# Hybrid encoder step on eight cores: weight conversion spread over two groups, casts on two more engines, eight PSUM banks for gate and up

## Time and profile before

| | |
|---|---|
| times of 3 runs | 7601.93, 8012.99 and 8454.6 us, median 8012.99 |
| profiled execution | 7586.13 us, span of its slowest core 7585.1 us |
| spans of the 8 cores | 7554.7 to 7585.1 us, granted clock 0.958 to 0.965 |
| first group (31.4 to 1022.7 us) | 991.3 us |
| fifth group, the same block number without conversion | 767.4 us |
| second group (1022.7 to 1821.9 us) | 799.2 us |
| last group, the sample tokens (from 6749 us) | 836.1 us |

### The profile page before, as it was taken

The page is one execution under the profiler, slowest core; times in us unless marked ns, Lnnn a source line. Parts: engine busy times, 40 slices in busy tenths (PEclk is TensorE's granted clock), DMA queues, the critical chain, the costliest instruction groups (busy, mean ns, idle before and its releaser), DMA issues.

```text
span 7585.1 us, 114887 instructions; the slowest of 8 cores (7554.7 to 7585.1 us)
## 1 busy us (share of the span) xinstructions
PE 6630.0 (87%) x39776; PEld 3525.2 (46%) x39776; DVE 2912.0 (38%) x5057; ACT 2651.3 (35%) x4204; POOL 1403.3 (19%) x1750
## 2 busy tenths in 40 slices
PE   5777788989899998989898989899999989896777
PEld 2333334454444445454444454544444454555666
DVE  4545534343333343333434343433343433433332
ACT  1412315151524335261414152524333351614343
POOL 1112111202111121212121212121121212122121
PEclk9899999999999999999999999999999999998888
DMA  8699762424233342424242424243343424256666
GB/s 264 216 310 306 224 206 85 146 86 157 97 121 122 115 154 69 147 73 160 97 146 98 158 89 142 95 148 116 109 134 103 148 70 149 77 181 213 208 222 200
DMA packets 452258, 1130.56 MB, mean 149 GB/s; under 512 B 38384, under 2 KB 166128, under 8 KB 451696
## 3 DMA queue, kind: packets, MB, share of 16 engines
q1 hardware_dynamic: 433568, 1059.23, 43.5%
q0 software_dynamic: 18128, 63.97, 2.2%
HBM read 973.12 MB, written 149.95 MB: 148 GB/s over the span
## 4 chain that ended last, share of the span: by engine, by line
PE 61%; DVE 11%; ACT 10%; issue 7%; DMA 5%; POOL 4%; SPq 2%; DVEq 0%; ACTq 0%; POOLq 0%
PE psb L542 14%; PE psb L522 12%; PE psb L518 11%; PE psb L756 5%; POOL tC L533 4%; PE psb L889 3%; PE psb L986 3%; PE psb L1007 3%; DVE tA L528 2%; PE psb L696 2%; ACT tA L531 2%; ACT eT L1065 2%; SPq L270 1%; PE psb L1166 1%; ACT tq L759 1%
## 5 line engine op out<-in xcount | busy, mean ns | idle before, releaser
L533 POOL TENSOR_TENSOR tC<-tA,rstdT 128x512 f32<-128x512 f32 (+1 forms) x792 | 954.4, 1205 | 4198.5 <-ACT tA L531 4081.0
L522 PE MATMUL psb<-hT,wring 128*128 128x512 bf16 (+1 forms) x6336 | 1430.9, 369 | 132.3 <-DVE BIG L536 126.6
L518 PE MATMUL psb<-hT,wring 128*128 128x512 bf16 (+1 forms) x6336 | 1434.5, 369 | 87.2 <-DVE tA L528 78.6
L542 PE MATMUL psb<-BIG,wring 128*128 128x512 bf16 (+1 forms) x6336 | 1322.5, 370 | 43.8 <-DVE wring L412 38.6
L531 ACT ACTIVATE tA<-tA 128x512 f32<-128x512 f32 (+1 forms) x792 | 479.8, 606 | 2218.3 <-DVE tA L528 2217.9
L536 DVE TENSOR_TENSOR BIG<-psb,tC 128x512 bf16<-128x512 f32 (+1 forms) x792 | 524.2, 662 | 1757.8 <-POOL tC L533 1757.8
L522 PEld LDWEIGHTS psb<-hT,wring 128*128 128x128 bf16 x6336 | 588.1, 98 | 895.0 <-issue 355.3
L518 PEld LDWEIGHTS psb<-hT,wring 128*128 128x128 bf16 x6336 | 618.9, 98 | 785.6 <-issue 133.4
L542 PEld LDWEIGHTS psb<-BIG,wring 128*128 128x128 bf16 x6336 | 621.1, 98 | 735.4 <-issue 76.9
L528 DVE TENSOR_TENSOR tA<-psb,rstdT 128x512 f32<-128x512 f32 (+1 forms) x792 | 515.7, 651 | 164.7 <-ACT rstdT L485 164.6
L994 ACT ACTIVATE eT<-psb 128x1024 bf16<-128x1024 f32 (+2 forms) x640 | 532.7, 892 | 106.4 <-PE psb L986 57.5
(11 more groups left out here) (179 smaller groups left out, 6233.0 us busy)
## 6 DMA issues: line engine op xcount, KB each, us to landing
wring<-wsc SPq DMA_DIRECT2D x1280, 512.0 KB, 3.9
wsc<-wring SPq DMA_DIRECT2D x160, 512.0 KB, 9.4
vb<-w_gate SPq DMA_DIRECT2D x66, 512.0 KB, 9.7
vb<-w_up SPq DMA_DIRECT2D x66, 512.0 KB, 10.7
vb<-w_down SPq DMA_DIRECT2D x66, 512.0 KB, 12.3
vb<-cbk SPq DMA_DIRECT2D x64, 512.0 KB, 5.1
vb<-cbv SPq DMA_DIRECT2D x64, 512.0 KB, 4.5
vb<-w_in SPq DMA_DIRECT2D x36, 512.0 KB, 11.6
```

The source lines that it names most:

```text
L518: P.add("pe", lambda kc=kc, bg=bg, wg=wg, fl=fl: nc.tensor.matmul(psb[bg][:, 0:T], wg[:, kc, fl * 128:(fl + 1) * 128], hT[:, kc, 0:T], sta ...
L522: P.add("pe", lambda kc=kc, bu=bu, wu=wu, fl=fl: nc.tensor.matmul(psb[bu][:, 0:T], wu[:, kc, fl * 128:(fl + 1) * 128], hT[:, kc, 0:T], sta ...
L533: P.add("pool", lambda ts=ts: nc.gpsimd.tensor_tensor(out=tC[ts][:, 0:T], in0=tA[ts][:, 0:T], in1=rstdT[:, 0:T], op=ALU.mult), [("t", ts, ...
L542: P.add("pe", lambda: nc.tensor.matmul(psb[ab][:, 0:T], wd[:, fl, dcl * 128:(dcl + 1) * 128], aT[:, fc, 0:T], start=(fc == 0), stop=(fc == ...
```

## The change

- Conversion goes over two groups. In the first group every tile is still loaded as float32 and cast, but only the `in` and `out` tiles and those with an even index (`written_first`, 104 of 168) are written to `wsc`. The second group fetches those 104 from `wsc`, and loads, casts and writes the other 64 (56 full and 8 half-sized) itself.
- The fetches of the second group are issued 2 tiles ahead in `first_pass`. From the third group on, nothing of this changes.
- The staging area grows: 12 halves in the first group (parts of `kbT` too, in two pieces of 512 columns), 8 in the second.
- Of the two halves of a tile, VectorE casts the first. The second is cast by ScalarE, for `in` and `out` tiles by GpSimd.
- Gate and up use all eight banks: chunk `fc` has the pair `2 * (fc % 4)`.
- `o_transpose` of group B is put off by 4 tiles for `i = 0` and 6 otherwise (before: 2, 4, 6 and 6 for the four block numbers), in bank 4 for `i` 0 and 1. The last head's is after unit 5 of group A (before: 3), in bank 7. In group A it stands ahead of the normalization of the fourth unit, not behind it.

```diff
@@ staging and the two groups
+    late = [k_ for k_ in parts if k_[0] == "k" or (k_[0] == "v" and k_[2] > 0)]
+    early = late + [k_ for k_ in parts if k_ not in late]
...
+    def written_first(tid):
+        (l, name, idx) = cat_list[tid][0]
+        return name in ("in", "out") or idx % 2 == 0
+
+    def converts(n):
+        return n < NW or (n < NCONV and not written_first(n % NW))
+
+    def writes_back(n):
+        return written_first(n % NW) if n < NW else converts(n)
...
     def first_cast(n):
...
+                if hf == 0:
+                    P.add("dve", lambda: nc.vector.tensor_copy(out=dst, in_=buf), tk, [("w", s)])
+                elif name in ("in", "out"):
+                    P.add("pool", lambda: nc.gpsimd.tensor_copy(out=dst, in_=buf), tk, [("w", s)])
+                else:
+                    P.add("act", lambda: nc.scalar.copy(out=dst, in_=buf), tk, [("w", s)])
...
+    def cast_to(m):
+        while fp["cast"] < min(m, NCONV):
+            if converts(fp["cast"]):
+                first_cast(fp["cast"])
+            fp["cast"] += 1
+
     def first_pass(n):
-        while fp["load"] < min(n + LOOK + 3, NFIRST):
-            while fp["cast"] <= min(fp["load"] - 4, n + LOOK):
-                first_cast(fp["cast"])
-                fp["cast"] += 1
-            first_load(fp["load"])
+        while fp["load"] < min(n + LOOK + 3, NCONV):
+            cast_to(min(fp["load"] - 3, n + LOOK + 1))
+            if converts(fp["load"]):
+                first_load(fp["load"])
             fp["load"] += 1
...
+        cast_to(n + LOOK + 1)
+        while fp["back"] < min(n + LOOK, NCONV):
+            if writes_back(fp["back"]):
+                first_back(fp["back"])
             fp["back"] += 1
+        while fp["fetch"] < min(n + LOOK + 1, NCONV):
+            if not converts(fp["fetch"]):
+                fetch(fp["fetch"])
+            fp["fetch"] += 1
@@ def ffn
-                bg, bu = rot(), rot()
+                bg = 2 * (fc % 4)
+                bu = bg + 1
@@ def attn_prompt
-        def o_transpose(half, hh):
-            bt = 6
+        def o_transpose(half, hh, bt):
...
-                    deferred.append([idx + min(nk // 2, 6), o_transpose, (1, h)])
+                    lag = 4 if i == 0 else 6
+                    deferred.append([idx + lag, o_transpose, (1, h, 6 if lag <= nk // 2 else 4)])
...
+            if u == 3 and hp > 0:
+                o_transpose(0, hp - 1, 6)
             if u % 2 == 1:
...
-            if u == 3 and hp > 0:
-                o_transpose(0, hp - 1)
...
-            if idx == 4:
-                flush(10 ** 9)
-        o_transpose(0, 3)
+            if idx == 6:
+                for d_ in deferred:
+                    d_[1](1, 3, 7)
+                deferred.clear()
+        o_transpose(0, 3, 6)
```

More of the change, by code:

```diff
@@ L367, in build @@
     cat_list = list(cat.items())
-    NFIRST = len(cat_list)
+    NW = len(cat_list)
+    NCONV = 2 * NW
     LOOK = 2
-    stage = []
+    parts = {}
     for l_ in range(2):
         for k_ in range(3):
[L373 to L379, removed]
-    fp_halves = {}
+            parts[("v", l_, k_)] = (
+                [vbt[l_][:, 4 + 4 * k_:8 + 4 * k_].rearrange("p a h b -> p (a h b)")[:, 0:2048].bitcast(F32)],
+                [("vb", l_, 4 + 4 * k_ + q) for q in range(4)])
+        parts[("a", l_)] = ([vat[l_][:, 4:8].rearrange("p a h b -> p (a h b)")[:, 0:2048].bitcast(F32)],
+                            [("va", l_, 4 + q) for q in range(4)])
+        for p_ in range(2):
+            parts[("k", l_, p_)] = ([kbT[l_][:, 2 * p_ + a_, 1024:2048].bitcast(F32) for a_ in range(2)],
+                                    [("kbx", l_, p_)])
+    late = [k_ for k_ in parts if k_[0] == "k" or (k_[0] == "v" and k_[2] > 0)]
+    early = late + [k_ for k_ in parts if k_ not in late]
+    fp = {"load": 0, "cast": 0, "back": 0, "fetch": 0, 0: 0, 1: 0}
+    fp_halves = {}
+    def written_first(tid):
[5 more added lines that the diff above has]
+        return written_first(n % NW) if n < NW else converts(n)
     def tile_nel(n):
-        (l, name, idx), tid = cat_list[n]
+        (l, name, idx), tid = cat_list[n % NW]
         if name[0] == "d":
@@ L440, in wload @@
         wcount[0] += 1
-        s = n % NSLOT
-        if n < NFIRST:
-            if cat_list[n][1] != tid:
-                raise ValueError("weight order")
+        if cat_list[n % NW][1] != tid:
+            raise ValueError("weight order")
+        if n < NCONV:
             first_pass(n)
-            return s
-        while fp["back"] < NFIRST:
-            first_back(fp["back"])
-            fp["back"] += 1
-        dma("sp", wring[:, s, 0:nel], wsc[tid][:, 0:nel], [("ws", tid)], [("w", s)], ("w", s))
-        return s
+        else:
+            fetch(n)
+        return n % NSLOT
     nstate = {"bank": None, "pend": []}
@@ L737, in qk_job @@
             FT = ("t", ts, "B")
+            xtok = []
             if kind == "ka":
```

58 lines of the change are left out of this document (34 added, 24 removed).

## The result

The changed kernel takes 7504.23, 7509.81 and 7523.17 us; the kernel before took 7591.33 and 7601.93 us beside it. The ratio is **0.9889, 95% interval 0.9855 to 0.9924**: a gain of 1.1%, which is real, but 7504 us lies outside the range of 7310 to 7485, and 123 us above the forecast. (In many executions of this program the cores of one die get a lower clock and take longer; the figures here are of executions, or of the four cores of a die, without that.)

A forecast was written before the change was run, and what follows sets the result against it. TensorE, busy 6630.0 of 7585.1 us, was taken to bound the kernel, the DMA engines parts of the first group. Terms -85 + 10 - 57 - 26 - 12 - 35 = -205 from 7586 gave 7381 us, range 7310 to 7485.

The forecast's parts named there:

- All is hidden behind the DMA-bound loads: 0: First group: casts moved from VectorE partly to ScalarE and GpSimd cost nothing, 0 us.
- The 64 VectorE and 56 ScalarE casts lie beside TensorE: Second group: casts add 7.5 us to VectorE's 27.64 and 10 us to ScalarE's 16.45 in a 79.40 us stage, beside TensorE.
- Writes leave the first group: First group: 31.5 MB no longer written in DMA-bound stages, -85 us, ends -79 and -100.
- Loads and writes in the second group: Second group: 31.5 MB more to read and 31.5 MB to write fits barely, +10 us, ends 0 and +111.
- the sign of the starved group: Second group, gate and up: TensorE waiting for `wring<-wsc` would show that slow fetches starve the group.
- The rival that starved it: Second group: full-queue slow landings hold there too, +111 for +10, giving 7482 us; chance 0.13.
- The rival that was slower than before: SyncE's queue, second group: loads over twice as long, 25 us, stretch all four ffns by 381 us, to 7752; chance 0.03.
- Eight banks, groups two to eight: Gate and up: the wait of line 522 for 536, at a stage's third chunk, goes entirely, -57 us.
- Eight banks, last group: Last group's gate and up: 55 waits on the late chain through ScalarE, GpSimd and VectorE go, -26 us.
- The rival that the waits only change their name: Gate and up: the chain or the four-slot weight ring holds TensorE as long; without the 83, 7464 us; chance 0.12.
- Group B, block 0: Attention: moved transposes shorten each head by 1.0 us in 12 periods, -12 us, ends 0 and -42.
- Group A: Attention: transposes moved ahead of line 1089 lose most of 41.1 us of waits, -35 us, ends 0 and -41.

The follow-up runs named there:

- Without the chain: Changed kernel with VectorE's up multiply of each chunk issued behind the gate multiply of the next: 7384.77 us, 7420.21 us in the profiled execution.
- the one-group version: Whole conversion back in the first group: 7474.86, 7484.51 and 7489.9 us from the changed kernel; 7429.84 and 7432.57 us with VectorE's up multiply also issued a chunk later.
- the banks-only one: Kernel before with the eight banks of gate and up alone, all else as before: 7529.57 to 7534.8 us in four runs.
- the chain apart and the loads earlier: Changed kernel, up multiply issued a chunk later, second group's loads two tiles earlier, fetches ahead of writes in SyncE's queue: 7371.62 and 7377.06 us, 0.9704 of before.

## Why the prediction was wrong

The step that failed is the one on the casts: **"All is hidden behind the DMA-bound loads: 0"** and **"The 64 VectorE and 56 ScalarE casts lie beside TensorE"**. It read the busy time of VectorE, 27.64 of 79.40 us, as slack. It was the idle time of a chain with a period of 3.52 us against 3.45 of TensorE, and had no slack at all. The profile before showed it, in VectorE's timeline in any gate and up stage; the prediction read that timeline for a head of attention and not here. What the casts cost in place of nothing is seen in the run without them: the second group is 84 us shorter there, 60 by medians.

Point by point, predicted and measured:

- *Writes leave the first group*: -85, measured -71.5 (-57 by medians). Without the chain it is -84.5 between the cores read and -76 by medians, so the bytes were priced nearly right, somewhat high. With the chain the gate and up stage stops at 100.3 us (forecast 91, measured 90.0 without the chain), where TensorE waits 17.4 us for `wring` of ScalarE's cast and the DMA share falls to 0.94.
- *Casts on two engines, first group*: 0. Gate, up and down of the first group take 688.3 us in the one-group version against 679.6 in the banks-only one: about +9. (The two also differ in the staging area, so not all of this need be the casts'.)
- *Loads and writes in the second group*: +10, measured +91.0 (+72 by medians). This is the largest miss. Both signs that the prediction named appeared: TensorE waits there for `wring<-wsc` (42.4 and 12.2 us), the sign of the starved group, and SyncE for ScalarE's cast, the sign of the loop. The rival that starved it (+111, for slow landings) had nearly the size, and half of the landings: the second fetch of a step lands after some 11 us, more than the 9.0 that the working allowed. It did not have the cause, for without the casts the same bytes go through in time. The rival that was slower than before had the right loop, write behind cast with load and fetch behind the write, but let a late landing start it. Here it hung on a cast that VectorE and ScalarE reached late. The bytes alone were priced right: without the casts the group takes 12 us more than without conversion (medians), and with the casts, the chain apart and the loads earlier 801.5 against 791.7 of the one-group version, +9.8 (+10 by medians).
- *Eight banks, groups two to eight*: -57, measured -57.4. The size is right by luck, the working is not: that VectorE and GpSimd "have slack" and the 0 for the down projection are both false. Gate and up fell by 15 a group, not 8, and down took 7 back. The recorded wait of 126.6 us was only a part of what the banks cost, and the chain's debt at the down projection, which cancelled the rest, was not in the sum.
- *Eight banks, last group*: -26, measured -1.1. Here the period is 2.24 us a chunk before and after, and what TensorE gains at gate and up (209.2 to 191.5) it waits out at down (91.6 to 107.7). Only without the chain does the group fall: to 810.0 us on the core read, by 26.1, and by 20 between medians (835.3 and 815.2). The rival that the waits only change their name was right for this group, and for nearly half of what gate and up gained in the others.
- *Group B, block 0*: -12, measured -14.2 (first and fifth group, 62.7 to 53.8 and 60.8 to 55.5 us). *Group A*: -35, measured -39.5 (486.0 to 446.5 us in eight groups). Both right, and in the trace of the transposes alone too.

Between the slowest cores the measured parts, -71.5 + 9 + 91.0 - 57.4 - 1.1 - 14.2 - 39.5, make -84; the profiled executions differ by -81.9. Of the 123 us missed, 81 are the second group, 25 the last, 13.5 the writes and 9 the casts in the first, less some 7 that attention gave more. That the kernel with the chain apart takes 7384.77 us, close to the forecast of 7381, is chance. There gate and up of groups three to eight gave 92 us (1925.7 to 1833.7), where the forecast had 48 for them, and the second group lost 32 to 52 us where it had 10.

## What to carry to other kernels

An engine's low busy share is slack only if its instructions don't wait for each other in a ring over several engines: read the timeline of one period in mid-stage, and compare it with the bound engine's period (3.52 against 3.45 us here) before anything is put on that engine. More buffers buy a lead and not a rate; ask where in the next stage the lead is paid back. In an in-order queue, whatever a write waits for is also waited for by the fetches behind it (SyncE's queue here: 291.5 us), so put the fetch ahead, and start loads early enough that no cast is on its last moment.

## What was not expected of the hardware

- A stage whose DMA engines are busy 0.76 of the time can be short of data: nothing was issued for 12 us (1251.3 to 1263.3) and then a burst, at 221 GB/s over the stage. In the same stage, with the loads earlier, they ran at 257 GB/s.
- Issuing costs SyncE time: four pieces into `kbT` take 2.36 us in its queue, one whole tile 0.34 us (both vary: the fetches shown take up to 0.84).
- The granted clock was 0.90 in the second group's stalled gate and up stage and 1.00 in the unstalled one of the fifth; with the earlier loads it was 0.98. The stall is paid once more in slower matmuls: the eight behind the wait of 3.16 us took 3.25 us, the next eight 1.89. For the same 354 matmuls TensorE was busy 85.52 us there and 76.20 in the fifth group, so some 9 of the 100.10 us are this (an estimate from the busy times).
